# Latent attention's scores in halves and quarters of the TensorE array, four heads at a time, with full 128-column transposes and every second head's probabilities scaled on POOL

## What is computed

```python
MLA_HEADS, MLA_NOPE, MLA_ROPE, MLA_VD = 16, 64, 32, 64      # a query or key has 96 elements a head

def mla_queries(cq, w_q_up, q_g):
    return rms_norm((cq @ w_q_up).reshape(B, L, MLA_HEADS, MLA_QK), q_g)

def mla_keys_values(ckv, kpe, w_kv_up, k_g):
    k_nope, v = kv[..., :MLA_NOPE], kv[..., MLA_NOPE:]
    k = rms_norm(jnp.concatenate([k_nope, k_pe], axis=-1), k_g)
    return k, v

def mha(q, k, v, scale):        # latent rows read 384 keys (128 cached, 256 latent), context rows their own 128
    a = softmax_f32(jnp.einsum('bqhd,bkhd->bhqk', qb, k), scale)
    return jnp.einsum('bhqk,bkhv->bqhv', a.astype(v.dtype), v)
```

## Time and profile before

| | |
|---|---|
| median of 3 runs | 1520.59 us (1519.58 to 1520.69) |
| the profiled execution's own time | 1519.7 us |
| its span | 1517.5 us |
| busy share of the span: PE, DVE, ACT, POOL | 99%, 71%, 44%, 2% |
| core of MLA, first scores to first matmul of `wo(1)` | 1146.83 to 1204.52 us |

### The profile page before, as it was taken

How to read it: one execution, slowest core, us unless ns; L and a number is a source line. 1 busy time by engine, 2 the same in 40 slices (tenths; PEclk the granted TensorE clock), 3 DMA queues, 4 the chain that set the end, 5 groups by cost and what they waited for, 6 DMA issues and landing times.

```text
span 1517.5 us, 21930 instructions
## 1 busy us (share of the span) xinstructions
PE 1509.8 (99%) x8854; PEld 1443.9 (95%) x8854; DVE 1080.2 (71%) x1738; ACT 668.4 (44%) x1030; POOL 31.8 (2%) x43
## 2 busy tenths in 40 slices
PE   9999999999999999999999999999999999999999
PEld 5999999988779999999999999999997899999999
DVE  5887887788687887886678887877588876443332
ACT  5433333254686633333363333325458765333221
POOL 0000000000021000000000000000020000000000
PEclk9999999999999999999999999999999999999999
DMA  9756566543224355655455656654331033433333
GB/s 390 279 212 233 208 245 225 187 152 117 92 70 157 136 217 212 228 199 183 164 197 184 233 203 224 220 195 147 115 130 57 1 136 115 139 112 139 99 131 118
DMA packets 52132, 258.00 MB, mean 170 GB/s; under 512 B 6592, under 2 KB 8896, under 8 KB 36800
## 3 DMA queue, kind: packets, MB, share of 16 engines
q1 hardware_dynamic: 49344, 252.61, 46.0%
q10 hardware_dynamic: 2688, 4.00, 0.8%
HBM read 253.29 MB, written 3.29 MB: 169 GB/s over the span
## 4 chain that ended last, share of the span: by engine, by line
PE 95%; DVE 1%; ACT 1%; DMA 1%; issue 1%; SPq 0%; POOL 0%; ACTq 0%; DVEq 0%; POOLq 0%
PE ps L2103 29%; PE ps L2104 29%; PE ps L2105 29%; PE ps L2744 1%; PE ps L2464 1%; PE ps L2635 1%; PE ps L2753 1%; PE ps L2767 1%; PE ps L2490 1%; DMA wm_first<-in_w_mod_first 1%; DMA w_raw<-in_w_in 0%; PE ps L2212 0%; DVE w_lo L1319 0%; PE ps L2428 0%; PE ps L2235 0%
## 5 line engine op out<-in xcount | busy, mean ns | idle before, releaser
L1319 DVE TENSOR_TENSOR w_lo<-w_raw,w_hi 128x2048 fp32r<-128x2048 f32 (+3 forms) x178 | 349.6, 1966 | 236.7 <-ACT w_hi L749 234.0
L2103 PE MATMUL ps<-hx_hi,w_hi 128*128 128x384 f32 (+1 forms) x1432 | 480.2, 335 | 0.1
L2104 PE MATMUL ps<-hx_lo,w_hi 128*128 128x384 f32 (+1 forms) x1432 | 478.6, 334 | 0.0
L2105 PE MATMUL ps<-hx_hi,w_lo 128*128 128x384 f32 (+1 forms) x1432 | 478.6, 334 | 0.0
L749 ACT ACTIVATE w_hi<-w_raw 128x2048 fp32r<-128x2048 f32 (+3 forms) x178 | 294.7, 1656 | 404.4 <-DMA w_raw<-in_w_out 214.4
L2103 PEld LDWEIGHTS ps<-hx_hi,w_hi 128*128 128x128 f32 x1432 | 268.9, 188 | 2.4 <-issue 1.8
L2104 PEld LDWEIGHTS ps<-hx_lo,w_hi 128*128 128x128 f32 x1432 | 268.9, 188 | 0.0
L2105 PEld LDWEIGHTS ps<-hx_hi,w_lo 128*128 128x128 f32 x1432 | 268.8, 188 | 0.0
L2105 PE MATMUL ps<-g_hi,w_lo 128*128 128x384 f32 x704 | 236.6, 336 | 0.0
L2103 PE MATMUL ps<-g_hi,w_hi 128*128 128x384 f32 x704 | 236.5, 336 | 0.0
L2104 PE MATMUL ps<-g_lo,w_hi 128*128 128x384 f32 x704 | 236.5, 336 | 0.0
(11 more groups left out here) (280 smaller groups left out, 1476.8 us busy)
## 6 DMA issues: line engine op xcount, KB each, us to landing
w_raw<-in_w_in SPq DMA_DIRECT2D x88, 1024.0 KB, 4.8
wm<-in_w_mod SPq DMA_DIRECT2D x128, 512.0 KB, 5.7
w_raw<-in_w_out SPq DMA_DIRECT2D x64, 704.0 KB, 4.1
w_raw<-in_w_qkv SPq DMA_DIRECT2D x12, 1024.0 KB, 4.7
wm_first<-in_w_mod_first SPq DMA_DIRECT2D x8, 1024.0 KB, 19.2
w_raw<-in_w_o SPq DMA_DIRECT2D x8, 1024.0 KB, 4.9
w_raw<-in_w_qup SPq DMA_DIRECT2D x8, 576.0 KB, 3.7
w_raw<-in_w_down SPq DMA_DIRECT2D x6, 704.0 KB, 3.9
```

The source lines that it names most:

```text
L1319: nc.vector.tensor_tensor(w_lo[:, slot, 0:width], w_raw[:, slot, 0:width], w_hi[:, slot, 0:width].bitcast(F32), ALU.subtract).then_inc(w_l ...
L2103: nc.tensor.matmul(out, l_hi, r_hi, start=first, stop=False)
L2104: nc.tensor.matmul(out, l_hi, r_lo, start=False, stop=False)
L2105: return nc.tensor.matmul(out, l_lo, r_hi, start=False, stop=last)
```

## The change

The queries and keys are kept apart: for all heads of a tile first the 64 nope elements, then the 32 rope elements. A transpose takes full 128 columns: two heads' nope parts, or four heads' rope parts. There are 24 turns in place of 28, and a turn of queries has three transposes in place of four. The transposed tiles are `mqN`, `mkN` (two heads above one another, 64 partitions each) and `mqR`, `mkR` (four heads, 32 partitions each; `mkN` and `mkR` are parts of the tensor `mkT`). A score is the sum of two matmuls in one PSUM bank: `scores_nope` with two heads side by side in the row halves of the array, and `scores_rope` with four heads in its row quarters. So four heads go together: `mla_head` and `mla_pieces` now give four units of kind 0, then four of kind 1. The orders on PE, ACT and DVE are rewritten for groups of four; of each group DVE scales units 0 and 2, and POOL units 1 and 3; `ma` has four buffers in place of two. The rope part of the second half of the keys is made on POOL in place of DVE.

```diff
-                    for i in range(4):
+                    for i in range(3 if t < 12 else 4):
                         if t < 12:
-                            src = mq[:, (t // 3) % 2, t % 3, i * QK:(i + 1) * QK]
+                            src = mq[:, (t // 3) % 2, i, (t % 3) * P:(t % 3 + 1) * P]
                         else:
...
+                            half, j = divmod(t - 12, 6)
+                            if j < 4:
+                                src = mk_nope(half, j)[:, i * P:(i + 1) * P]
+                            else:
+                                src = mk_rope(half, 2 * (j - 4) + i % 2)[:, (i // 2) * P:(i // 2 + 1) * P]
+                        mm = nc.tensor.transpose(ps[:, TURN_BANK[t], i * P:(i + 1) * P], src, ident[:])
```

```diff
         def mla_head(u):
-            return 2 * (u // 4) + u % 2
+            return 4 * (u // 8) + u % 4
         def mla_pieces(u):
-            return PIECES[(u // 2) % 2]
+            return PIECES[(u // 4) % 2]
...
+                def scores_nope(g, half):
+                    u0 = 4 * g + 2 * half
+                    if g:
+                        pe.wait_ge(mexp_done, mla_exps(u0 - 3))
+                    for i, piece in enumerate(mla_pieces(u0)):
+                        for u in (u0, u0 + 1):
+                            pair = mla_head(u) // 2
+                            scores_of(u, mqN[:, pair, :], mkN[:, pair, :], slice(NOPE * (u % 2), NOPE * (u % 2 + 1)), *piece,
+                                      i == 0, False)
+                def scores_rope(g):
+                    for i, piece in enumerate(mla_pieces(4 * g)):
+                        for u in range(4 * g, 4 * g + 4):
+                            quad = mla_head(u) // 4
+                            mm = scores_of(u, mqR[:, quad, :], mkR[:, quad, :], slice(ROPE * (u % 4), ROPE * (u % 4 + 1)),
+                                           *piece, False, i == len(mla_pieces(u)) - 1)
+                            if i == len(mla_pieces(u)) - 1:
+                                mm.then_inc(ms_ready, 1)
```

On PE the groups, and before them the turns that stand ahead of group 1's scores:

```diff
+                scores_rope(0)
                 turn_of(10)
+                pe.wait_ge(mheads, 4)
                 pe.wait_ge(*turned(9))
                 turn_of(11)
...
+                pe.wait_ge(*turned(10))
+                turn_of(18)
+                pe.wait_ge(*turned(11))
+                turn_of(19)
...
+                for g in range(U // 4):
+                    if g:
...
+                        values(2 * g - 2)
+                    if g < U // 4 - 1:
+                        scores_nope(g + 1, 0)
+                    if g:
...
+                        values(2 * g - 1)
+                    turn(4 * g)
+                    turn(4 * g + 1)
...
+                    if g < U // 4 - 1:
+                        scores_nope(g + 1, 1)
+                        scores_rope(g + 1)
+                    turn(4 * g + 2)
+                    turn(4 * g + 3)
```

On ACT, on DVE and on POOL:

```diff
+                for g in range(U // 4):
+                    evac_aT(4 * g)
+                    evac_aT(4 * g + 1)
...
+                    evac_aT(4 * g + 2)
+                    if g < U // 4 - 1:
+                        exps(4 * g + 4)
+                    evac_aT(4 * g + 3)
...
+                    elif g == 2:
+                        high_half(PHASE["wo", 1][0], 1)
+                    if g < U // 4 - 1:
+                        for u in range(4 * g + 5, 4 * g + 8):
+                            exps(u)
...
+                    top(4 * g)
...
+                    top(4 * g + 1)
+                    scale(4 * g)
+                    top(4 * g + 2)
+                    scale(4 * g + 1)
...
+                    if g >= 2 and g % 2 == 0:
+                        out_copy(g - 2)
+                    top(4 * g + 3)
+                    scale(4 * g + 2)
+                    scale(4 * g + 3)
+                    if g >= 2 and g % 2 == 0:
+                        out_copy(g - 1)
...
+            for u in range(1, 2 * MLA_HEADS, 2):
+                pool.wait_ge(ri_odd, u // 2 + 1)
+                if u >= 4:
+                    pool.wait_ge(mt_ready, u - 3)
+                for j, (qb, at, slots) in enumerate(mla_pieces(u)):
+                    cols = slice(at, at + len(slots) * P)
+                    ins = nc.gpsimd.tensor_scalar(ma[:, u % 4, cols], me[:, u % 4, cols], ri[:, u % 4, j:j + 1], None, ALU.mult)
+                ins.then_inc(ma_odd, 1)
```

More of the change, by code:

```diff
@@ L117, in build_step @@
         with ExitStack() as part:
-            mk1a = sb("mk1a", [P, 3, 8, QK], where=part)
+            mk1a = sb("mk1a", [P, 3, 8 * QK], where=part)
         with ExitStack() as part:
@@ L123, in build_step @@
         with ExitStack() as part:
-            mk1b = sb("mk1b", [P, 8, QK], where=part)
+            mk1b = sb("mk1b", [P, 8 * QK], where=part)
         with ExitStack() as part:
@@ L228, in build_step @@
             mv_all = sb("mv_all", [P, 4, D], where=part)
-            mqT = sb("mqT", [QK, MLA_HEADS, T], where=part)
+            mqN = sb("mqN", [P, MLA_HEADS // 2, T], where=part)
+            mqR = sb("mqR", [P, MLA_HEADS // 4, T], where=part)
             kpe = sb("kpe", [P, 4, ROPE], where=part)
@@ L242, in build_step @@
             kvr = sb("kvr", [P, NB], where=part)
[L243 removed]
+            mkT = sb("mkT", [P, 16, ROW], where=part)
             with ExitStack() as part2:
[L246 removed]
+                mk0 = sb("mk0", [P, 4, 8 * QK], where=part2)
                 mq = sb("mq", [P, 2, NB, T], where=part2)
@@ L2729, in mla @@
                 turn_of(13)
-                for t, free in ((14, 6), (15, 7), (16, 8), (17, 12), (18, 13), (19, 14)):
-                    pe.wait_ge(*turned(free))
-                    turn_of(t)
-                pe.wait_ge(mheads, 4)
+                pe.wait_ge(mheads, 3)
+                pe.wait_ge(mv_done, 7)
+                turn_of(8)
+                pe.wait_ge(*turned(6))
+                turn_of(14)
+                pe.wait_ge(*turned(7))
+                turn_of(15)
+                pe.wait_ge(mkheads, 1)
@@ L2734, in mla, with scores_of @@
+                pe.wait_ge(*turned(8))
+                turn_of(16)
                 pe.wait_ge(*turned(15))
+                turn_of(17)
+                pe.wait_ge(*turned(16))
                 turn_of(9)
                 U = 2 * MLA_HEADS
-                def scores(u):
-                    h = mla_head(u)
-                    if u >= 4:
-                        pe.wait_ge(mexp_done, mla_exps(u - 4))
-                    for qb, at, slots in mla_pieces(u):
-                        n = len(slots) * P
-                        mm = nc.tensor.matmul(ps[:, u % 4, at:at + n], mqT[:, h, qb * P:(qb + 1) * P],
-                                              mkT[0:QK, h, slots[0] * P:slots[0] * P + n], start=True, stop=True)
-                    mm.then_inc(ms_ready, 1)
+                def scores_of(u, qT, kT, rows, qb, at, slots, start, stop):
+                    n = len(slots) * P
+                    return nc.tensor.matmul(ps[:, u % 4, at:at + n], qT[rows, qb * P:(qb + 1) * P],
+                                            kT[rows, slots[0] * P:slots[0] * P + n], start=start, stop=stop)
@@ L2784, in mla @@
+                pe.wait_ge(kbank_free, 4)
+                scores_nope(0, 1)
+                pe.wait_ge(*turned(16))
+                pe.wait_ge(*turned(17))
+                scores_rope(0)
                 turn_of(10)
+                pe.wait_ge(mheads, 4)
                 pe.wait_ge(*turned(9))
                 turn_of(11)
[L2787 to L2805 removed]
+                pe.wait_ge(k0_keys, 2)
```

253 lines of the change are left out of this document (133 added, 120 removed).

## The result

The changed kernel takes **1534.88 us** (median of 5 runs, 1534.11 to 1535.09) against 1519.72 for the kernel before (5 runs, 1519.58 to 1520.69): ratio 1.0097, 95% interval 1.0085 to 1.0108. It is 15.2 us slower, where +11.3 was forecast, and the time lies inside the predicted range.

A forecast was written before the change was run, and what follows sets the result against it. PE's own work was taken to bound the kernel before, and a loop of waits the changed core. Terms -0.65 + 0 + 2.0 + 4.7 + 7.8 - 2.5 = +11.3 us on 1519.7 gave 1531.0, median 1532, range 1524 to 1540.

The forecast's parts named there:

- The bound, and the direction: MLA core: PE's own work sets the pace; matmul time saved (0.76 us a group) goes into switches (0.90), so slower.
- Quarters overlap fourfold: Rope scores: four heads in row quarters take the time of one, 0.87 or 0.65 us.
- The rival of half overlap: Rope scores: quarters overlap only as halves, a rope block costs twice, +6 us, 1538; chance 0.08.
- nothing is buffered: Steady core: four banks serve four units released together, so a group's period is a loop, 8.2 or 7.5 us.
- the walk: Core: a group's loop added up engine by engine from trace costs, 8.2 us for even groups and 7.5 for odd.
- The odd groups: Groups followed from the first maxima of one-piece units to the next group's: 7.5 us each.
- the step for units 4 to 28: Three groups of each kind plus ACT's extra work, 49.3 us against 41.5 before: +7.8 us.
- Units 0 to 4: Start of the core: turns 18 and 19 wait for ACT's copies behind exponentials, 10.0 us against 5.3: +4.7.
- the clock falls: Core: PE idles some 1.5 us in 8 and drops to 1.2 GHz, +20 us or more, over 1550; chance 0.03.
- First maxima: Core start, first scores to first maxima: 3.2 us against 1.2 before, +2.0.
- Tail: Unit 28's maxima to the core's end: 7.2 us against 9.7 before, -2.5, taking POOL's scaling as 0.7.
- Turns: Transposes of queries and keys ahead of the core: -0.65 us between projections, 0 just ahead of the core.

The follow-up runs named there:

- e7: Kernel before, with value matmuls on both sides of the next scores at five places, ten more array mode changes and the same work: 1521.21 us.
- e4: Changed kernel without the rope score matmuls, so a piece of the computation is left out: 1526.95 us, ratio 1.0048 to the kernel before.
- e6: Changed kernel with DVE taking the fourth unit's maxima ahead of splitting a pair of heads: 1535.1 us, ratio 1.0101 to the kernel before.
- e9: Changed kernel with a group's first exponentials on ACT moved ahead of the copy of the last group's third unit: 1536.85 us.
- e3: Changed kernel with rope scores right behind each nope half, releasing units two by two, with a second rope block a group: 1542.9 us.
- e11: Changed kernel's tiles, worked by pairs of units, DVE scaling all, copies of turns 10 and 11 first, both exponentials ahead of both probability copies: 1524.85 us.
- e5: Changed kernel with ACT's copies of turns 10 and 11 ahead of the exponentials of units 0 and 1: 1532.98 us.
- e1: Changed kernel with all probabilities scaled on DVE, none on POOL: 1535.8 us, ratio 1.0107 to the kernel before.
- e8: Changed kernel with the edits of e1, e5 and e6 together: 1532.27 us, ratio 1.0084 to the kernel before.
- e12: As e11, but with every second unit scaled on POOL: 1528.8 us, ratio 1.0057 to the kernel before.
- e2: Kernel before, with every second unit scaled on POOL, that part of the change alone: 1524.45 us, ratio 1.003.

## Why the prediction was right, and where its sizes were off

**The bound, and the direction: right.** PE's own work rose from 6.40 to 6.55 us a group where 6.54 was forecast, so the matmul time saved does go into switches. e7 measures a switch between the full array and the column halves alone at 0.17 (the term was 0.15); the term of 0.2 for a row mode is what a nope block shows, which takes 0.85 where its matmuls cost 0.65. The Trainium skill's rule that changing the tiling mode drains TensorE (TensorEngine Tiling, Key Properties) agrees with e7 in direction; the size is from the runs alone.

**Quarters overlap fourfold: right.** Four heads' rope block takes 0.86 us where two heads' nope block takes 0.85. The rival of half overlap is refuted, by the trace of the changed kernel. The Trainium skill's measured speedup of 3.07 for four row tiles (TensorE: Matmul & The Clock Gate, Measured speedup vs the span model) does not show here: a rope block is not 0.2 us longer than the halves' block.

**The loop, "nothing is buffered": right.** Groups came 8.09 apart where 8.2 was walked. e4 and e6 add that the walk took one chain for the loop where several nearly tie: shortening DVE's part, or dropping the rope block, brought a fraction of its length.

The odd groups took 7.99, not 7.5. The walk had ACT go from maxima to exponentials at once; in the trace, a copy of probabilities stands ahead of them (1196.82), which waits for transposes that PE has behind the rope block. So the exponentials start 1.10 us behind the maxima, not 0.55, and PE goes on at 2.86, where the walk had 2.3; the 5.13 us behind it are as walked (5.2). e9 does not speak against this: it left the same two copies ahead of the second exponentials. That term, 3 x 0.5, is more than the whole error of the step for units 4 to 28 (+8.7 against +7.8). The even groups gave back 3 x 0.1, and ACT's extra work cost 1.9 (8.97 and 8.94 against 7.99) where 2.2 was taken. That step came out closer than its parts.

**Units 0 to 4: under-sized by 1.6.** The chain of copies behind exponentials was there: the second copy is done 4.84 us behind the first maxima, 4.9 by the walk, and PE waited 2.8 + 0.7 us. What I left out is the clock: of the rival "the clock falls" I had said that it would come in the steady part and cost over 20 us. It came once, behind the longest wait, for some 3.4 us, and not in the steady part, where PE idles at most 1.8 us at a time (granted clock 1.00). At half speed, 3.4 us of work is 1.7 longer than it need be, about the size of the miss. That the steady part kept the full clock was luck as much as judgment: in e3's profiled execution the clock fell there too, at 1198.0, behind a wait of 1.65 us.

**First maxima: right** (+1.9 against +2.0). **Tail: -1.8, not -2.5.** The term for POOL's scaling was 0.7 us; it measured 1.24, and 0.6 for the small form, so it was just above the upper bound from the earlier trace rows, and in the tail PE waited for it twice, 0.53 and 0.74 us. **Turns: -0.5 together, not -0.65.** Both errors are small.

**The total.** These terms miss by 3.3 us of the 3.9 between +11.3 and +15.2, all but that of the first maxima to the same side; the rest lies ahead of the MLA, where single executions differ by 1 us. The 0.9 that the forecast of 1532 added for the median was chance: with two more runs the median of the kernel before is 1519.72, the profiled execution's own time.

**Where the 15 us are.** In the changed kernel the layout costs PE little: 8 x 0.15 = 1.2 us of work in the groups, against the 28 transposes saved. Its 15 us are PE's idleness in the core (14.1 us in place of 0.6) and the 1.7 us of low clock. e11 shows that this idleness does not come with the tiles: with the same tiles and transposes its core takes 63.1 us and PE never waits in the steady part. It is 4.7 us slower than the kernel before, and that is PE's own work, a second rope block and its switch for every four units.

Against e11 the changed kernel loses 10.0 us: by stretches 6.5 in units 0 to 4 and 4.0 in units 4 to 28, with 0.7 given back in the tail (a joint release shifts some of this to the first stretch, since unit 4's maxima come with those of units 5 to 7). Between the two lie the joint release of four units from four banks, the order of the queues around it, and the copies of turns 10 and 11, which with the clock are 2.3 us by e5. POOL is no part of it: by e1 it gives about 1 us. How much is the release and how much the order is open, since no run kept the joint release with every queue re-ordered for it (e5, e6 and e9 changed one place each, e8 two and the scaling). None of the versions with the new layout beats the kernel before: the best is 0.32% slower.

## What to carry to other kernels

When tiles of the array are packed with work from several units, ask which buffers must be free at one moment and which come full at one moment. If that is all of them, double buffering is gone, and its loss is counted in waits per round, not in matmul time. Count mode changes per round before counting the columns saved. And walk each in-order queue for a copy ahead of a producer: two lines in ACT's order were worth 13 us here. Moving such a copy pays only if it leaves the place ahead of the instruction that the loop waits for, as e11 did and e9 did not. Where waits let the granted clock fall, look at it before pricing a stage: 3.4 us at the lower level cost about 1.7 here, where the waits that e5 removed were worth 0.8. Moving work to a slower engine is free only where the bound engine waits anyway: the changed kernel gains 1 us by it, e12 loses 4.

## What the runs showed of the hardware

A scaling of 128x384 f32 by a scalar of each partition took 1.24 us on POOL, where DVE's row in the kernel before gives 0.42, and twice it took 2.14, both times while DVE ran the subtraction of two tensors (L1397). I had expected 0.7. In groups by form (total us and mean ns of one, then idle time ahead):

```profile
L784 POOL TENSOR_SCALAR ma<-me,ri 128x384 f32<-128x384 f32 x16 | 21.8, 1360 | 43.7 <-DVE ri L2101 43.6
```

In all eight runs that scale on POOL, this form took 2.14 us wherever it lay beside that subtraction for 1.03 us, and 1.62 for an overlap of 0.51 (e2); beside the split's subtraction (L2118 here), one input of which lies in PSUM, it took 1.24. That DVE's instruction is the cause is still argued from this coincidence; no run moved it.
